# Four norms of a two-block transformer kernel computed in two token halves, with the last output panels and the first feed-forward group split the same way

## The reference

```python
def hybrid_layer(x, ...):                      # block a, two layers
    ...                                        # attention and retention branches, gated, give `mixed`
    x = x + mixed @ w_out
    h2 = rmsnorm(x, g_mlp)
    x = x + jnp.square(jax.nn.relu(h2 @ w_up)) @ w_down
    return x
...
for l in range(DEPTH):                         # block b, two layers
    y = hybrid_mixer(x, ...)                   # ends in merged @ w_out + b_out
    x = layer_norm(DN_ALPHA * x + y, ln1_g[l], ln1_b[l])
    y = conv_ffn(x, w_up[l], conv_w[l], conv_b[l], w_down[l])
    x = layer_norm(DN_ALPHA * x + y, ln2_g[l], ln2_b[l])
```

## Time and profile before

| | |
|---|---|
| median of 3 runs | 3595.11 us (3594.56 to 3597.14) |
| the profiled execution | 3596.14 us; its span from first to last instruction 3594.4 us |
| PE busy in the span | 3444.3 us (96%) |
| DVE, ACT, POOL busy | 1591.8, 1432.2, 1445.8 us (44, 40, 40%) |
| mean granted TensorE clock | 0.985 of full speed |
| HBM read | 294.34 MB, 82 GB/s over the span |

### The profile page before, as it was taken

How to read it: one execution, slowest core, us unless ns; L and a number is a source line. 1 busy time by engine, 2 the same in 40 slices (tenths; PEclk the granted TensorE clock), 3 DMA queues, 4 the chain that set the end, 5 groups by cost and what they waited for, 6 DMA issues and landing times.

```text
span 3594.4 us, 45460 instructions
## 1 busy us (share of the span) xinstructions
PE 3444.3 (96%) x16338; PEld 2792.4 (78%) x16338; DVE 1591.8 (44%) x2423; ACT 1432.2 (40%) x2114; POOL 1445.8 (40%) x1100
## 2 busy tenths in 40 slices
PE   7999999999999999999999999999999999999997
PEld 6788778887688778887768876787777688767785
DVE  5724232226623332227861444434478514344435
ACT  4735233224734332224462444333344534353333
POOL 3334444444334444444323342444343233434442
PEclk9999999999999999999999999999999999999999
DMA  3121222222112222222212121222212121222221
GB/s 142 59 83 71 94 93 95 93 95 94 69 72 91 91 88 94 94 105 73 83 36 83 68 88 71 94 93 93 82 72 71 54 75 61 95 69 94 93 93 59
DMA packets 43812, 298.49 MB, mean 83 GB/s; under 512 B 4816, under 2 KB 5456, under 8 KB 8592
## 3 DMA queue, kind: packets, MB, share of 16 engines
q1 hardware_dynamic: 41696, 291.52, 22.7%
q10 hardware_dynamic: 1968, 4.94, 0.4%
HBM read 294.34 MB, written 2.10 MB: 82 GB/s over the span
## 4 chain that ended last, share of the span: by engine, by line
issue 54%; POOL 32%; PE 11%; DVE 1%; ACT 1%; POOLq 1%; DVEq 0%; ACTq 0%
POOL w_lo L310 32%; PE ps L432 4%; PE ps L434 3%; PE ps L433 3%; PE ps L516 0%; POOLq L305 0%; DVE arena L1640 0%; ACT arena L1115 0%; POOLq L309 0%; DVE x L1675 0%; DVE arena L1663 0%; DVE tmp L1470 0%; ACT y_hi L1134 0%; DVE x L1912 0%; ACT x L1433 0%
## 5 line engine op out<-in xcount | busy, mean ns | idle before, releaser
L310 POOL TENSOR_TENSOR w_lo<-w_raw,w_hi 128x512 fp32r<-128x512 f32 x1096 | 1445.6, 1351 | 2106.1 <-ACT w_hi L936 2106.1
L432 PE MATMUL ps<-x_hi,w_hi 128*128 128x512 f32 x2752 | 1098.9, 399 | 23.0 <-DVE x_lo L1455 18.4
L433 PE MATMUL ps<-x_lo,w_hi 128*128 128x512 f32 x2752 | 1076.8, 391 | 0.0
L434 PE MATMUL ps<-x_hi,w_lo 128*128 128x512 f32 x2752 | 1076.7, 391 | 0.0
L936 ACT ACTIVATE w_hi<-w_raw 128x1024 fp32r<-128x1024 f32 x548 | 547.5, 1048 | 503.9 <-PE ps L434 503.9
L432 PEld LDWEIGHTS ps<-x_hi,w_hi 128*128 128x128 f32 x2752 | 519.9, 189 | 172.2 <-issue 38.1
L434 PEld LDWEIGHTS ps<-x_hi,w_lo 128*128 128x128 f32 x2752 | 519.7, 189 | 111.3
L433 PEld LDWEIGHTS ps<-x_lo,w_hi 128*128 128x128 f32 x2752 | 520.4, 189 | 106.0 <-issue 2.4
L432 PE MATMUL ps<-y_hi,w_hi 128*128 128x512 f32 x1248 | 490.9, 393 | 20.4 <-DVE x L1675 13.0
L433 PE MATMUL ps<-y_lo,w_hi 128*128 128x512 f32 x1248 | 487.1, 390 | 0.0
L434 PE MATMUL ps<-y_hi,w_lo 128*128 128x512 f32 x1248 | 486.7, 390 | 0.0
(11 more groups left out here) (184 smaller groups left out, 3139.0 us busy)
## 6 DMA issues: line engine op xcount, KB each, us to landing
w_raw<-stream SPq DMA_DIRECT2D x274, 1024.0 KB, 4.8
x<-x_t SPq DMA_DIRECT2D x4, 512.0 KB, 5.7
rotary<-rot ACTq DMA_DIRECT2D x4, 512.0 KB, 3.6
y_t<-x SPq DMA_DIRECT2D x8, 256.0 KB, 2.1
ct<-consts ACTq DMA_DIRECT2D x2, 770.0 KB, 4.7
arena<-pos ACTq DMA_DIRECT2D x2, 256.0 KB, 3.4
vec<-vectors ACTq DMA_DIRECT2D x4, 116.0 KB, 2.0
ct<-consts ACTq DMA_DIRECT2D x1, 128.0 KB, 4.1
```

What stands on the lines that cost most here:

```text
L310: ins = nc.gpsimd.tensor_tensor(WL[:, s, c:c + S], RAW[:, s, c:c + S], WH[:, s, c:c + S].bitcast(F32), ALU.subtract)
L432: pe.matmul(ps, wh, xh, start=(k == 0), stop=False)
L433: pe.matmul(ps, wh, xl, start=False, stop=False)
L434: return pe.matmul(ps, wl, xh, start=False, stop=last)
```

## The change

At all four places, the norm is computed for tokens 0 to 255 and 256 to 511 apart (`HS`), and matrix work is laid beside it:

- The last two `wo` panels (`gemm_halves`) run all four tiles for the first token half, then all four for the second: eight passes of 24 products 256 wide. Small products of the first half's norm stand between the passes of the second half (`beside`).
- Group 0 of the feed-forward layer (`first_up`) runs four passes of 48 products 256 wide, over token half h and panel p. In block b the order is (h, p) = (0,0), (0,1), (1,0), (1,1): both panels with the first half, then both with the second. In block a it is (0,0), (1,0), (0,1), (1,1): each panel with both halves. The second half's norm has its small products between these passes.
- The instructions of the norm on DVE and ACT are 256 wide and twice as many. The constant products that stood in these norms are gone. In block b the squares go to eight tiles of their own.
- `ring[0] = 4` is now set before the `gb`, `wb` and `wo` panels, so these tiles go round four banks instead of two.
- `hi` of the panels around is placed anew in ACT's order; `hi_first` and `hi_part` split one panel's two instructions.
- In block a, the negated sinks are computed after the norm `n1` instead of before it; in the first layer that is where DVE waits for the vectors' DMA.

```diff
+HS = (slice(0, S // 2), slice(S // 2, S))
+HN = S // 2
...
+            def gemm_halves(n, xh, xl, name, beside):
+
+                banks = [next_bank(name(j)) for j in range(4)]
+                for h in range(2):
+                    for j in range(4):
+                        s = (n + j // 2) % 2
+                        if h == 0 and j % 2 == 0:
+                            pe.wait_ge(lo_ready, n + j // 2 + 3)
+                        T.after(("read",) + name(j) + (0,) if h else bank_reader[banks[j]], own=False)
+                        for k in range(KD):
+                            c = (k * 2 + j % 2) * P
+                            mm = split_products(PS[:, banks[j], HS[h]], k, k == KD - 1, WH[:, s, c:c + P], WL[:, s, c:c + P],
+                                                xh[:, k, HS[h]], xl[:, k, HS[h]])
+                        T.done(mm, *name(j), h)
...
+                        if (h, j) in beside:
+                            beside[h, j]()
...
-            def mixer_gemms(l, w, t, gates):
-
+            def mixer_gemms(l, w, t, gates, beside):
+
+                ring[0] = 4
...
+                def first_up():
+
+                    if l or t == "b":
+                        pe.wait_ge(up_read, base_t)
+                    for h, p in ((0, 0), (1, 0), (0, 1), (1, 1)) if t == "a" else ((0, 0), (0, 1), (1, 0), (1, 1)):
+                        if h == 0:
+                            pe.wait_ge(lo_ready, ff + p + 3)
+                            T.after(*bank_reader[2 * p:2 * p + 2], own=False)
+                        s = (ff + p) % 2
+                        for k in range(KD):
+                            if p == 0:
+                                T.after(h_ready(k, h), own=False)
+                            for m in range(2):
+                                c = (k * 2 + m) * P
+                                mm = split_products(PS[:, 2 * p + m, HS[h]], k, k == KD - 1, WH[:, s, c:c + P],
+                                                    WL[:, s, c:c + P], XH[:, k, HS[h]], XL[:, k, HS[h]])
+                                if h and k == KD - 1:
+                                    mm.then_inc(up_full, 1)
+                            if (h, p, k) in beside:
+                                beside[h, p, k]()
...
-                mixer_gemms(l, w, t, gates)
-                ring[0] = 4
-                inverse_deviation(6, t, l, "n2")
-                ffn(l, t, w["ff"], FF1_GROUPS, 4, *bases(t, l), lambda k: (t, l, "h2_lo", k))
...
+                mixer_gemms(l, w, t, gates, {(1, 0): lambda: deviation(0), (1, 1): lambda: spread_half(0)})
+                ffn(l, t, w["ff"], FF1_GROUPS, 4, *bases(t, l), lambda k, h: (t, l, "h2_lo", k, h),
+                    {(0, 0, 2): lambda: deviation(1), (0, 0, 6): lambda: spread_half(1)})
...
+                mixer_gemms(l, w, t, gates, {(1, 0): lambda: mean(0), (1, 2): lambda: mean_square(0)})
+                ffn(l, t, w["ff"], FF2_GROUPS, 2, *bases(t, l), lambda k, h: (t, l, "ln1_lo", k, h),
+                    {(0, 0, 6): lambda: mean(1), (0, 1, 7): lambda: mean_square(1)})
...
+                hi(w["wo"] + 2)
+                hi(w["wo"] + 3)
+                warm_root()
+                half_squares(0)
+                hi(w["ff"])
+                half_root(0)
+                half_x(0, 0)
+                half_x(0, 1)
+                hi_first(w["ff"] + 1)
+                half_x(0, 2)
+                half_x(0, 3)
+                hi_part((w["ff"] + 1) % 2, 1)
+                for k in range(4, KD):
+                    half_x(0, k)
+                half_squares(1)
+                half_root(1)
+                for k in range(KD):
+                    half_x(1, k)
```

More of the change, by code:

```diff
@@ L919, in _ @@
+                bank_reader[5] = (t, l, "ln2_root")
+                if l + 1 < DEPTH:
+                    keep_clock(4, 5)
         @block.scalar
@@ new lines, in half_squares, with half_root @@
+                def half_squares(h):
+                    for k in range(KD):
+                        A.after((t, l, "ln1_centered", k, h), ("read", t, l, "wb", 7))
+                        A.done(act.activation(AR[:, 20 + k, HS[h]], X[:, k, HS[h]], ACT.Square), t, l, "ln1_sq", k, h)
+                def half_root(h):
+                    A.after((t, l, "ln1_ms", h), "eps")
+                    A.done(act.activation(TMP[:, 3, HS[h]], PS[:, 5 + 2 * h, 0:HN], ACT.Sqrt, scale=1.0 / D, bias=ST[:, 97:98]),
+                           t, l, "ln1_root", h)
@@ new lines, in _ @@
+                for k in range(KD):
+                    A.after((t, l, "ln1_lo", k, 0), (t, l, "ln1_lo", k, 1))
+                    A.done(act.activation(X[:, k, :], X[:, k, :], ACT.Copy, scale=DN_ALPHA), t, l, "x2_scaled", k)
+                ffn(l, t, w["ff"], FF2_GROUPS, 2, *bases(t, l))
+                for _ in squares(lambda k: X[:, k, :], KD, lambda k: TMP[:, k % 2, :], lambda k: (t, l, "ln2_centered", k),
+                        lambda k: (t, l, "ln2_ms", k - 2) if k >= 2 else None, (t, l, "ln2_sq")):
+                    pass
@@ new lines, in _ @@
+                warm_root()
+                root(PS[:, 5, :], D, LN_EPS, (t, l, "ln2_root"), [(t, l, "ln2_ms"), "eps"])
+                if l + 1 < DEPTH:
+                    hi(at_b(l + 1)["iq"] + 1)
+                for k in range(KD):
+                    g = VB["ln2_g"] + k
+                    A.after((t, l, "ln2_scaled", k))
+                    A.done(act.activation(X[:, k, :], X[:, k, :], ACT.Identity, scale=VEC[:, l % 2, g:g + 1],
+                                          bias=VEC[:, l % 2, g + 8:g + 9]), t, l, "ln2_x", k)
+                    if l + 1 < DEPTH:
+                        split_hi(XH[:, k, :], X[:, k, :], [], (t, l + 1, "x_hi", k))
@@ new lines, in _ @@
+                centred(1)
+                half_inverse(1)
+                half_tiles(1, 0, 1, 2, 3, 4, 5, 6, 7)
+                half_lo(1, 7)
+                ffn(l, t, FF2_GROUPS, 2, *bases(t, l), x_sums(t, l, "ln2"))
+                for k in range(KD):
+                    V.after((t, l, "ln2_mean"), own=False)
+                    V.done(dve.scalar_tensor_tensor(X[:, k, :], PS[:, 4, :], -1.0 / D, X[:, k, :], ALU.mult, ALU.add),
+                           t, l, "ln2_centered", k)
+                inverse_root([(t, l, "ln2_root")])
@@ new lines, in _ @@
+                marks[(t, l, "ln2_inverse")] = ("dve", V.n)
+                for k in range(KD + 1):
+                    if k < KD:
+                        V.after((t, l, "ln2_sq", k), (t, l, "ln2_inverse"), own=False)
+                        V.done(dve.tensor_tensor(X[:, k, :], X[:, k, :], TMP[:, 3, :], ALU.mult), t, l, "ln2_scaled", k)
+                    j = k - 1
+                    if k and l + 1 < DEPTH:
+                        lo(XL[:, j, :], X[:, j, :], XH[:, j, :], [(t, l + 1, "x_hi", j)], (t, l + 1, "x_lo", j), own=False)
```

303 lines of the change are left out of this document (211 added, 92 removed).

## The result

The changed kernel takes 3616.8 us (median of four runs, 3615.6 to 3618.9), the kernel before 3596.1 (3594.6 to 3597.2, beside it): a ratio of 1.0058, with a 95% interval of 1.0041 to 1.0076. It is slower by 20.7 us, beyond the 0.2% named ahead; 3612 was forecast.

What follows compares the result with a forecast made beforehand. TensorE, busy 96% of the span, was taken as the bound, so its waits and product pace count. 3594.4 - 10.8 - 2.0 + 9.2 + 20.7 = 3611.5 us span, forecast 3612 us, range 3598 to 3626.

Steps and rivals of the forecast that it cites:

- Banks, -10.8: Into `wb` and `wo`: four banks instead of two remove TensorE's bank waits, -2.7 us each, -10.8 in all.
- start, -2.0: First norm `n1`: DVE's first sum no longer stands behind the sinks waiting for the vectors, -2.0 us.
- Block a, +9.2: Norm in block a: group 1 at t = 58.4 (t from third `wo` panel's start), +4.6 us, twice.
- The waiting for GpSimd: Block a's first half: some twelve DVE instructions meet POOL, about 0.4 us each, 5 us; without any waiting, cost 0.
- Block b, +20.7: Norms in block b: second half's chain serial, group 1's panel late; +11.4 and +9.3 us in the two layers.
- the second reciprocal: Block b, second half's norm: reciprocal expected at t = 54, t counted from the third `wo` panel's start.
- ScalarE's last rounding: Block b, second half's k-steps: ACT's last rounding at t = 64.8, 9.8 us later than before.
- the wait for `w_lo`: Block b before group 1: TensorE waits about 6.5 us for POOL's `w_lo`.
- the clock's: Block b, first layer: TensorE restarts low after standing; 2 us of that reach the sums of squares.
- The first, no contention: VectorE isn't held by GpSimd in the halves: block a costs 0, block b 7.2 each; no change; chance 0.20.
- The second, an overlap of the halves: Second half's chain advances under first half's passes: 5.8 and 14.2 us gained, twice each; 3542; chance 0.08.
- the third: Clock falls in all four norms: 4 us more in block a, 2 in block b; 3624; chance 0.10.

## Why the prediction was right, and where its sizes were off

**Banks, -10.8, and start, -2.0.** Right: 12.2 together by the medians, 11.4 before the third panels in the trace, and the first sum came 2.6 us earlier.

**Block a, +9.2.** Right in size: group 1 at t = 57.9 and 58.4 for 58.4, so +8.5 on the forecast's own base of 53.8, and the pass (1, 0) paced at 0.92 for 0.95. The 8.2 of the medians is another difference, against whole norms with the banks, where the trace has 5.7; that it lies near 9.2 is partly luck. The waiting for GpSimd was to be all of the 4.6 per block (0 without any of it). With the subtractions freed, 2.3 and 4.2 came back in the trace, 2 by the medians. Sums and the diagonal still have two SBUF inputs there, so a rest can be theirs; that wasn't tried. One step was wrong: "The pass (0,1), which could cover the second half's chain, stands behind it, and that is what the order costs". With that pass as cover group 0's passes end only 1.5 and 2.7 us earlier, and group 1's panel is rounded 4.3 later. The order costs nothing; it saves.

**Block b, +20.7.** The right mechanism, and 25.5 by the medians. Of its points the first half's start (37.3, measured 37.2), the second reciprocal (54, measured 55.8), ScalarE's last rounding (64.8, and in the first layer two more by the clock; measured to end at 67.6 and 65.7), the wait for `w_lo` (6.5, measured 6.1) and group 1 in both layers (80.6 and 78.5, measured 81.0 and 79.1) stand. The term that was mis-sized is the clock's: two us were counted behind the first wait, and none behind the second. After the 6.1 us for `w_lo` group 1 starts at 1.2 GHz, in both layers; in the earlier trace rows it started at full pace. From group 1 to the first product of `ln2`'s mean in the last layer are 351.5 us (3234.90 to 3586.37, the first row below), where the kernel with block a's halves alone takes 349.5 (the other two rows).

```profile
3586.37 1.10 PE L538 MATMUL ps<-tmp,ct 128*128 128x512 f32 x2 [2.27 <-DVE tmp L1616]
```

```profile
3213.65 0.39 PE L433 MATMUL ps<-x_hi,w_hi 128*128 128x512 f32 x1
...
3563.13 1.93 PE L538 MATMUL ps<-tmp,ct 128*128 128x512 f32 x2 [2.27 <-DVE tmp L1603]
```

Seven kernels with the wait of 6.1 take 351.5 to 351.9 there, four with whole norms 349.3 to 349.5. That is 2 us; taken for both layers, an estimate of 4 from the clock. Group 1 itself starts 0.4 and 0.6 later than forecast. Together 5.0, where the medians miss 4.8. All of it as one sum from the trace: -2.6 for the start, -11.4 before the third panels, +8.5 and +21.4 from there to group 1 in blocks a and b, +4 for the clock, 19.9; the medians have 20.7. (One small slip in the working: the terms given for the end of the `wo` passes in block b add up to 27.9, not 28.3. Measured is 28.4, and nothing else hangs on it.)

**The rivals.** The first, no contention, falls by 0.69 against 0.42. The second, an overlap of the halves, decides in block a before t = 33.7 and in block b before 55: measured are 39.3 (476.11) and 67.2, and both attempts to bring block b's nearer left it above whole norms. Of the third, a part came. The clock did fall in all four places. In block b it cost the 2 us a layer that this rival has over the forecast. In block a it fell for a few us only, and the second half's passes, paced at 0.92, then ran at the full clock, so its 4 us a layer there did not come.

**The best version** is that with banks and start alone: 3583.1 us, 0.34% below the kernel before and 34 us below the changed kernel.

## What to carry to other kernels

Before splitting a norm in halves, look in every queue it uses where the second half's chain stands. Here it stood behind the first half's last tile on VectorE and ScalarE, so it was serial, and the halves only lengthened it. Behind such a chain look at what the same queue does next: the panel for the next group stood there, and its delay set group 1's start in block b. A change that bundles a small sure gain (banks that alternate, an early start) with a large uncertain one is best run in parts at once: the small part alone was the best kernel.

## What was not expected of the hardware

**The clock behind a wait of TensorE.** 18 constant products, 36 records, in a wait of 8.8 us kept the granted clock at 1.00 over the 1.1 us that were left of it; without them it was 0.52 in the six us behind the wait.

**The same code, some us apart.** Between group 1 in the second block a and the third `wo` panel in the first block b these kernels are the same, 868 us of it. It took 864.96 us in the run with the rescaling on VectorE, first below, and 871.24 in that with the other order and the early inverse:

```profile
1302.72 0.40 PE L433 MATMUL ps<-x_hi,w_hi 128*128 128x512 f32 x1
2167.68 0.28 PE L433 MATMUL ps<-x_hi,w_hi 128*128 128x256 f32 x1
```

```profile
1307.92 0.49 PE L433 MATMUL ps<-x_hi,w_hi 128*128 128x512 f32 x1 [3.22 <-POOL w_lo L311]
2179.16 0.28 PE L433 MATMUL ps<-x_hi,w_hi 128*128 128x256 f32 x1
```

The changed kernel took 868.08. Some 1.7 of the second one's 6.3 us more follow directly on its wait of 3.2 us, again at the lower clock. The rest that was looked at is also TensorE's clock, low for a few us in one trace and not in another at the same instructions. These are the second one and the run with the other order alone, in `wb`:

```profile
1886.00:1888.00 2.00, 2.00 (x6) 1.52 (x6) 0.00 (x0) 2.00 (x5) 0.00 (x0) 0.50 0.00 0
```

```profile
1886.00:1888.00 2.00, 2.00 (x9) 1.65 (x10) 0.00 (x0) 2.00 (x4) 0.00 (x0) 1.00 0.00 0
```

TensorE was busy without a gap in both for the 5 us before. So a difference of a few us between the spans of two profiles says nothing of an edit. Within a norm kernels with the same code agree better: group 1 of block b starts at t = 80.1 to 81.3 in the first layer of five of them, and at 79.1 to 79.9 in the second. Why the clock falls in one trace and not in the other stays open.
